# The store of the relative-bias rows is issued one weight piece later in the SyncE order

## The chip, the cores and the metric

The program runs on one core of one Trainium2 chip. The metric is device time in microseconds (us). Engines are TensorE (PE for its matmuls, PEld for its weight loads), VectorE (DVE), ScalarE (ACT), GpSimd (POOL) and SyncE (SP), which here only issues DMAs.

## What is computed

One layer of a hybrid decoder trunk on x of 512 tokens by 1024 channels, float32. The normalised input is multiplied by one wide projection `w_in`, whose columns feed three token mixers (A: sparse attention with a low-rank K/V and an indexer, B: gated DeltaNet, C: compressed, selected and window attention) and three merge gates. Their outputs go through `w_branch`, the gates and `w_out`, and are added to x. All softmax attention shares one relative-bias table:

```python
h = rms_norm(x, norm_g[l])
proj = h @ w_in[l]
a_part, b_part, c_part, gate_part = split_cols(proj, (...))
...
bias = jnp.transpose(bias_tab[t5_bucket(dist)], (0, 3, 1, 2))     # 32 buckets x 8 heads
logits = jnp.einsum('bqhd,bqkhd->bhqk', qb, kg) * scale + bias
...
x = x + (merged @ w_out[l])
```

## The kernel before

**Weights.** The projection is cut into chunks of up to 512 columns, and each chunk into four pieces (0 to 3), each with 2 of the 8 blocks of 128 rows (an exception are the two `phi` chunks, not touched here). The chunks at the start are C0 (448 columns), C1 (460), A0 (384), QI (512) and A2 (328), in that order, so the running piece number n is 0 to 3 for C0, 4 to 7 for C1, 8 to 11 for A0 and 12 to 15 for QI.

**The way of a piece.** SyncE loads piece n into one of three `stage` buffers (`load`, L449); from n = 3 on it first waits until the low split of piece n - 3 has been made (`lo_ready`), which is when that buffer comes free. ScalarE scales the piece in place (two ACTIVATEs, L738) and writes its float16 high part to `w_hi` (L746, which also waits for one of six `w_hi`/`w_lo` pairs to come free). GpSimd then writes the low part, `stage - w_hi`, to `w_lo` (L520). TensorE multiplies: a chunk is four tiles (t = 0 to 3), each tile eight k-steps of three matmuls (L1626, L1627, L1628: high by high, high by low, low by high), and k-steps 2j and 2j + 1 use piece j. So a tile has 24 matmuls and a chunk 96, and the first tile of a chunk waits for the low part of each of its pieces (`ready_pair`).

**Order on ScalarE.** Everything is in program order. `drain_chunk` copies a tile's bank out (L729) and then prepares pieces of the next chunk: after tile 0 its piece 0, after tile 1 its piece 1, after tile 2 its pieces 2 and 3, after tile 3 nothing (`FOLLOW`). The banks of the tiles alternate between two. GpSimd follows the same table; after the low splits of C1 it squares the C0 results (L537, L539).

**The relative-bias rows.** In the third gap of chunk C0 TensorE multiplies the table by a one-hot matrix (L1688, two products), VectorE scales the result into `rel_row` (8 partitions by 640 floats, L1086) and increments `rows_ready` (L1089). SyncE waits for this, stores the rows 16 times over to the DRAM tensor `rel_rows` (L480, 320 KB) and later, from piece QI,0 on, after the wait for `row_stored`, reads them back shifted into `strips` (L486, eight loads, one ahead of each of eight weight pieces). The other waits for `row_stored` and `strips_loaded` stand on VectorE ahead of the `ukv` copies in chunk A2 (L1177), on GpSimd (L615) and on VectorE (L1429), all later.

SyncE's queue is written out by hand: a wait in it holds back every load that stands behind it.

Of the kernel before, what the change touches and what calls it, by code (L numbers as in the profile page):

```python
# [127 lines left out]
def trunk(nc, x, norm_g, w_in, a_kv_norm, a_w_ukv, a_q_norm, a_k_norm, b_conv, b_a_log, b_dt_bias, b_out_norm,  # L128
# [9 lines left out]
    with ctx:  # L138
# [237 lines left out]
        for c, j in order:  # L376
            phi_piece = CHUNKS[c][0] == "phi"
            pieces.append((c, j, n_phi if phi_piece else n_pairs))
            n_phi, n_pairs = n_phi + phi_piece, n_pairs + (not phi_piece)
        piece_at = {(c, j): n for n, (c, j, _) in enumerate(pieces)}  # L380
        pair_at = {(c, j): k for c, j, k in pieces if CHUNKS[c][0] != "phi"}
        split_chunks = [c for c in range(len(CHUNKS)) if CHUNKS[c][0] != "phi"]
# [35 lines left out]
        def piece_view(t, c, n_rows=2):  # L418
            n = CHUNKS[c][2]
            return t[:, 0:n_rows * n].rearrange("p (k n) -> p k n", k=n_rows)  # L420
# [4 lines left out]
        @block.sync  # L425
        def _(sp):
            def load_x(t):
                sp.dma_start(x_in[t], x[0, t * P:(t + 1) * P, :]).then_inc(x_loaded[t], 16)

            def twice(row):  # L430
                return row.unsqueeze(1).to_broadcast([row.shape[0], 2, 64])

            def halves(row, n):
                return par_rows[row:row + n, :].rearrange("r (a d) -> r a d", a=2)

            def load(n):
                c, j, k = pieces[n]
                src, c0, width = CHUNKS[c]
                if n >= STAGES:
                    pc, _, pk = pieces[n - STAGES]  # L440
                    sp.wait_ge(phi_used if CHUNKS[pc][0] == "phi" else lo_ready, pk + 1)
                if src == "phi":
                    dst = piece_view(stage[:, n % STAGES, :], c, 4)
                    ap = c_phi_w1[0, c0].rearrange("(k p) n -> p k n", p=P)[:, 4 * j:4 * j + 4, :]
                else:
                    dst = piece_view(stage[:, n % STAGES, :], c)
                    ap = {"w_in": w_in, "w_branch": w_branch, "w_out": w_out}[src][0].rearrange(
                        "(k p) n -> p k n", p=P)[:, 2 * j:2 * j + 2, c0:c0 + width]
                sp.dma_start(dst, ap).then_inc(w_loaded[n % STAGES], 16)  # L449

            load_x(0)
            load_x(1)
            load(0)
            load(1)
            load_x(2)
            load_x(3)
            load(2)
            for src, dst in (
                (b_conv[0].rearrange("w (m p) -> (w m) p", p=P), par_rows[R_CONV:R_CONV + 48, :]),
                (a_kv_norm, par_rows[R_CKV:R_CKV + 1, :]),  # L460
                (twice(a_q_norm), halves(R_AQ, 1)), (twice(a_k_norm), halves(R_AK, 1)), (twice(c_q_norm), halves(R_CQ, 1)),
                (twice(c_k_norm[0]), halves(R_CK, 3)),
                (b_out_norm, par_rows[R_BOUT:R_BOUT + 1, :]),
                (c_cmp_pos[0].rearrange("v (c a) d -> (v c) (a d)", a=2), par_rows[R_POS:R_POS + 32, :]),
            ):
                sp.dma_start(dst, src).then_inc(in_loaded, 16)
            for src, dst in (
                (floats[:, F_HOT:F_HOT + S_REL], hot),
                (rel_bias, rel33[0:N_BUCKETS, :]),
                (b_dt_bias.to_broadcast([P, 4]), dt_b), (b_a_log.to_broadcast([P, 4]), neg_exp_a),  # L470
                (c_phi_w2[0].rearrange("v (k p) n -> p (v k) n", p=P), phi2),
            ):
                sp.dma_start(dst, src).then_inc(const_loaded, 16)
            sp.dma_start(ukv, a_w_ukv[0]).then_inc(ukv_loaded, 16)

            for n in range(STAGES, piece_at[CH_WO0, 0]):
                if n == piece_at[CH_C1, 3]:

                    sp.wait_ge(rows_ready, 1)
                    sp.dma_start(rel_rows, rel_row.unsqueeze(1).to_broadcast([N_HEADS, ROW_COPIES, S_REL])).then_inc(row_stored, 16)  # L480
                h = n - piece_at[CH_QI, 0]
                if 0 <= h < P // ROW_COPIES:

                    if h == 0:
                        sp.wait_ge(row_stored, 16)
                    sp.dma_start(strips[ROW_COPIES * h:ROW_COPIES * (h + 1), :, :],  # L486
                                 bass.AP(rel_rows.tensor, P - 1 - ROW_COPIES * h,
                                         [[S_REL - 1, ROW_COPIES], [ROW_COPIES * S_REL, N_HEADS], [1, T]])).then_inc(strips_loaded, 16)
                if n == piece_at[CH_A0, 2]:
                    sp.dma_start(mask_halves, masks).then_inc(masks_loaded, 16)  # L490
                load(n)

            sp.wait_ge(y_ready, NT * 2)
            sp.dma_start(x_again, x[0].rearrange("(t p) d -> p t d", p=P)).then_inc(x_reloaded, 16)
            for n in range(piece_at[CH_WO0, 0], len(pieces)):
                load(n)
            for n in range(2):
                for t in range(NT):
                    sp.wait_ge(out_ready, NT * n + t + 1)
                    sp.dma_start(out[0, t * P:(t + 1) * P, 512 * n:512 * n + 512],  # L500
                                 x_again[:, t, 512 * n:512 * n + 512]).then_inc(out_stored, 16)
            sp.wait_ge(out_stored, 16 * 2 * NT)
# [1585 lines left out]
```

## Time and profile before

| | us |
|---|---|
| median of 3 runs | 647.11 |
| the three runs | 2108.56, 643.32, 647.11 |
| profiled execution, its own time | 644.06 |
| span of its trace | 641.9 |
| mean granted TensorE clock, share of full speed | 0.981 |

The span is what the instructions cover; 2.2 us of the profiled execution's own time lie around it. Times in the rows below count from the start of the span.

### The profile page before, as it was taken

The page shows a single profiled execution, that of the slowest core. Times are in us where ns is not written, and L with a number is a line of the kernel's source. Part 1 is how long each engine was busy: PE and PEld are TensorE (multiplying, and loading weights), DVE is VectorE, ACT ScalarE, POOL GpSimd, SP SyncE. Part 2 cuts the span into 40 slices and gives each one's busy share as a digit, 9 for nine tenths or more (in the row PEclk, how much of TensorE's full clock was granted, in tenths as well). Part 3 has the DMA queues.
Part 4 walks back from the last instruction along what each step waited for, and adds up shares of the span by engine and source line. Part 5 has one row for each costly group of instructions (what it writes and reads, how often), then busy time and mean ns, then how long its engine had stood idle before and what let it go on. Part 6 is the DMA issues. An engine that isn't in the chain of part 4 may idle for free.

```text
span 641.9 us, 10022 instructions
## 1 busy us (share of the span) xinstructions
PE 585.5 (91%) x3763; PEld 365.5 (57%) x3763; DVE 395.0 (62%) x894; ACT 324.8 (51%) x578; POOL 222.7 (35%) x161
## 2 busy tenths in 40 slices
PE   3969997999999988799999999999999898799997
PEld 2424555756547754577777777765555555333443
DVE  6401477461577985886886556628799786477311
ACT  4634654434688868450712413257676767244510
POOL 0133452352225384142433430233313473132520
PEclk9998998999999899799999999999999999999999
DMA  8254783554213331220211020121111221072411
GB/s 321 70 127 110 152 135 99 149 148 130 67 26 83 124 100 34 66 66 2 62 37 34 13 88 1 34 67 51 54 63 34 67 66 46 21 242 83 135 50 49
DMA packets 31168, 53.04 MB, mean 83 GB/s; under 512 B 2743, under 2 KB 13201, under 8 KB 31121
## 3 DMA queue, kind: packets, MB, share of 16 engines
q1 hardware_dynamic: 30961, 52.27, 28.4%
q8 instruction: 30, 0.49, 0.3%
q14 instruction: 17, 0.14, 0.1%
q10 hardware_dynamic: 160, 0.14, 0.1%
HBM read 49.98 MB, written 2.42 MB: 82 GB/s over the span
## 4 chain that ended last, share of the span: by engine, by line
PE 68%; DVE 13%; ACT 8%; issue 5%; DMA 2%; POOL 2%; SPq 2%; DVEq 0%; ACTq 0%; POOLq 0%
PE bank L1813 13%; PE bank L1626 11%; PE bank L1628 10%; PE bank L1627 10%; PE bank L1885 5%; PE bank L1881 5%; PE bank L1883 5%; ACT stage L738 3%; DMA stage<-in_w_in 2%; PE bank L1662 2%; POOL w_lo L520 2%; PE bank L1705 2%; PE bank L2011 1%; ACT w_hi L746 1%; PE bank L1784 1%
## 5 line engine op out<-in xcount | busy, mean ns | idle before, releaser
L520 POOL TENSOR_TENSOR w_lo<-stage,w_hi 128x1024 f16<-128x1024 f32 (+4 forms) x76 | 149.1, 1963 | 242.4 <-ACT w_hi L746 242.4
L1813 PE MATMUL bank<-work 128*128 128x128 f32 x616 | 79.6, 279 | 8.1 <-DVEq L1319 7.9
L1813 PEld LDWEIGHTS bank<-work 128*128 128x128 f32 x616 | 76.8, 193 | 16.7 <-DVEq L1319 9.9
L746 ACT ACTIVATE w_hi<-stage 128x1024 f16<-128x1024 f32 (+4 forms) x76 | 74.5, 981 | 21.1 <-issue 17.2
L738 ACT ACTIVATE stage<-stage,small 128x512 f32<-128x512 f32 (+4 forms) x120 | 73.6, 662 | 7.8 <-DMA stage<-in_w_in 7.7
L1881 PE MATMUL bank<-hT_hi,w_hi 128*128 128x512 f16 x192 | 73.3, 382 | 1.7 <-PE bank L1885 0.9
L1883 PE MATMUL bank<-hT_lo,w_hi 128*128 128x512 f16 x192 | 73.3, 382 | 0.5 <-PE bank L1628 0.5
L1885 PE MATMUL bank<-hT_hi,w_lo 128*128 128x512 f16 x192 | 73.1, 381 | 0.3 <-PE bank L1628 0.2
L1626 PE MATMUL bank<-w_hi,hT_hi 128*128 128x260 f16 (+4 forms) x192 | 62.8, 327 | 9.4 <-POOL w_lo L520 6.4
L1627 PE MATMUL bank<-w_lo,hT_hi 128*128 128x260 f16 (+4 forms) x192 | 62.6, 326 | 0.0
L1628 PE MATMUL bank<-w_hi,hT_lo 128*128 128x260 f16 (+4 forms) x192 | 62.4, 325 | 0.0
L1626 PE MATMUL bank<-hT_hi,w_hi 128*128 128x512 f16 (+1 forms) x128 | 47.4, 371 | 6.2 <-DVE work L1140 3.8
L1344 DVE COPY_PREDICATED work<-level_masks,bank 128x512 f32<-128x512 uint8 x48 | 35.2, 734 | 23.6 <-PE bank L1813 17.4
L1628 PE MATMUL bank<-hT_hi,w_lo 128*128 128x512 f16 (+1 forms) x128 | 47.4, 370 | 0.0
L1627 PE MATMUL bank<-hT_lo,w_hi 128*128 128x512 f16 (+1 forms) x128 | 47.2, 369 | 0.0
L913 ACT ACTIVATE late<-late,small 128x128 f32<-128x128 f32 (+3 forms) x48 | 26.8, 557 | 30.7 <-DVE small L1427 30.7
L763 ACT ACTIVATE early<-bank 128x512 f32<-128x512 f32 x12 | 7.1, 591 | 61.8 <-PE bank L1885 61.8
L1626 PEld LDWEIGHTS bank<-w_hi,hT_hi 128*128 128x128 f16 x192 | 19.6, 102 | 24.4 <-POOL w_lo L520 7.3
L1227 DVE SCALAR_TENSOR_TENSOR bank<-qkvT,par,bank 128x512 f32<-128x512 f32 x36 | 27.0, 755 | 7.6 <-ACT bank L828 6.1
L1626 PE MATMUL bank<-strips,w_hi 128*128 128x512 f16 x64 | 25.1, 392 | 4.3 <-DVE strips L1533 1.5
L1881 PEld LDWEIGHTS bank<-hT_hi,w_hi 128*128 128x128 f16 x192 | 19.0, 99 | 15.7 <-issue 4.2
L1885 PEld LDWEIGHTS bank<-hT_hi,w_lo 128*128 128x128 f16 x192 | 18.9, 98 | 14.5 <-issue 2.0
(322 smaller groups left out, 1173.5 us busy)
## 6 DMA issues: line engine op xcount, KB each, us to landing
stage<-in_w_in SPq DMA_DIRECT2D x40, 512.0 KB, 3.5
stage<-in_c_phi_w SPq DMA_DIRECT2D x8, 512.0 KB, 3.9
stage<-in_w_branch SPq DMA_DIRECT2D x8, 512.0 KB, 3.7
stage<-in_w_out SPq DMA_DIRECT2D x8, 512.0 KB, 3.8
stage<-in_w_in SPq DMA_DIRECT2D x8, 260.0 KB, 2.8
strips<-rel_rows SPq DMA_DIRECT2D x8, 256.0 KB, 6.7
late<-in_x SPq DMA_DIRECT2D x1, 2048.0 KB, 10.3
out_x<-late SPq DMA_DIRECT2D x8, 256.0 KB, 2.0
```

Of the source, the lines that this page charges most:

```text
L520: gp.tensor_tensor(piece_view(w_lo[:, k % PAIRS, :], c), piece_view(stage[:, piece_at[c, j] % STAGES, :], c), piece_view(w_hi[:, k % PAIRS ...
L738: ins = nc.scalar.activation(full[:, r, :], full[:, r, :], ACT.Copy, scale=g_w[:, 2 * j + r:2 * j + r + 1])
L746: nc.scalar.activation(piece_view(w_hi[:, k % PAIRS, :], c), full, ACT.Copy).then_inc(hi_ready, 1)
L1227: ins = ve.scalar_tensor_tensor(acc, qkvT[:, m, w:w + T], tap[w], acc, ALU.mult, ALU.add)
L1344: return ve.copy_predicated(dst, level_masks[:, n, :].unsqueeze(1).to_broadcast([P, 4, P]), src)
L1626: mm(ps, lhs[0], rhs[0], start=start, stop=False)
L1627: mm(ps, lhs[0], rhs[1], start=False, stop=False)
L1628: return mm(ps, lhs[1], rhs[0], start=False, stop=stop)
L1813: ins = mm(ps[:, h * P:(h + 1) * P], lhs(h), rhs(h), start=True, stop=True)
L1881: mm(G.bank(g)[:, :], w[0], h[0], start=k == 0, stop=False)
L1883: mm(G.bank(g)[:, :], w[0], h[1], start=False, stop=False)
L1885: ins = mm(G.bank(g)[:, :], w[1], h[0], start=False, stop=k == KC - 1)
```

## The change

The wait for `rows_ready` and the store stood ahead of the load of piece 7, which is (C1, 3). They now stand ahead of the load of piece 8, which is (A0, 0). Nothing else differs, and no instruction is added or removed.

```diff
             for n in range(STAGES, piece_at[CH_WO0, 0]):
-                if n == piece_at[CH_C1, 3]:
+                if n == piece_at[CH_A0, 0]:
 
                     sp.wait_ge(rows_ready, 1)
                     sp.dma_start(rel_rows, rel_row.unsqueeze(1).to_broadcast([N_HEADS, ROW_COPIES, S_REL])).then_inc(row_stored, 16)
```

SyncE's order from piece 6 on was: load 6, wait and store, load 7, load 8, load 9, masks, load 10, load 11, first strip load, load 12. It is now: load 6, load 7, wait and store, load 8, and so on.

## Rows read from the trace of the kernel before

**Rows 1.** The page: TensorE's busy share, and the chain's shares.

```profile
PE 585.5 (91%) x3763; PEld 365.5 (57%) x3763; DVE 395.0 (62%) x894; ACT 324.8 (51%) x578; POOL 222.7 (35%) x161
...
PE 68%; DVE 13%; ACT 8%; issue 5%; DMA 2%; POOL 2%; SPq 2%; DVEq 0%; ACTq 0%; POOLq 0%
```

**Rows 2.** TensorE's waits from 30 to 130 us: total, times, longest.

```profile
PE bank L1626 <- POOL w_lo L520: 5.7, 1, 5.7
PE bank L1626 <- DVE work L1140: 3.8, 1, 3.8
```

**Rows 3.** Timeline of TensorE, 38 to 67 us: start, duration, instruction.

```profile
38.49 0.35 PE L1626 MATMUL bank<-w_hi,hT_hi 128*128 128x460 f16 x1 [0.30 <-PE bank L1628]
...
41.80 0.36 PE L1628 MATMUL bank<-w_hi,hT_lo 128*128 128x460 f16 x1
47.89 0.57 PE L1626 MATMUL bank<-w_hi,hT_hi 128*128 128x460 f16 x1 [5.73 <-POOL w_lo L520]
...
65.45 0.36 PE L1628 MATMUL bank<-w_hi,hT_lo 128*128 128x460 f16 x1
66.11 0.32 PE L1626 MATMUL bank<-w_hi,hT_hi 128*128 128x384 f16 x1 [0.30 <-PE bank L1628]
```

**Rows 4.** Timeline of GpSimd: low splits of pieces 4, 6, 7 and 8.

```profile
26.40 1.93 POOL L520 TENSOR_TENSOR w_lo<-stage,w_hi 128x920 f16<-128x920 f32 x1 [7.48 <-ACT w_hi L746]
...
35.92 1.93 POOL L520 TENSOR_TENSOR w_lo<-stage,w_hi 128x920 f16<-128x920 f32 x1 [2.13 <-ACT w_hi L746]
45.91 1.92 POOL L520 TENSOR_TENSOR w_lo<-stage,w_hi 128x920 f16<-128x920 f32 x1 [8.06 <-ACT w_hi L746]
...
52.92 1.64 POOL L520 TENSOR_TENSOR w_lo<-stage,w_hi 128x768 f16<-128x768 f32 x1 [2.67 <-ACT w_hi L746]
```

**Rows 5.** Timeline of ScalarE: pieces 6 and 7, a drain, piece 8.

```profile
34.87 0.97 ACT L746 ACTIVATE w_hi<-stage 128x920 f16<-128x920 f32 x1 [0.79 <-ACT stage L738]
43.58 1.25 ACT L738 ACTIVATE stage<-stage,small 128x460 f32<-128x460 f32 x2 [7.74 <-DMA stage<-in_w_in]
44.86 0.97 ACT L746 ACTIVATE w_hi<-stage 128x920 f16<-128x920 f32 x1
...
50.41 0.55 ACT L729 ACTIVATE raw_c<-bank 128x460 f32<-128x460 f32 x1 [4.14 <-PE bank L1628]
50.86 1.11 ACT L738 ACTIVATE stage<-stage,small 128x384 f32<-128x384 f32 x2
52.00 0.84 ACT L746 ACTIVATE w_hi<-stage 128x768 f16<-128x768 f32 x1
```

**Rows 6.** SyncE's own waits, 0 to 110 us.

```profile
SPq L480 <- DVEq L1089: 15.0, 1, 15.0
```

**Rows 7.** Timeline of SyncE: the store and loads 7 to 9.

```profile
34.15 0.75 SPq L480 DMA_DIRECT2D rel_rows<-work  x1
34.94 6.27 SPq L449 DMA_DIRECT2D stage<-in_w_in  x3
```

**Rows 8.** L449 from 34 to 50 us (four loads): issue durations, landing times.

```profile
L449 SPq DMA_DIRECT2D stage<-in_w_in x4: 368/1660/2864, 34.9 to 47.9; - x4
...
DMA to landing us min/median/max: 3.2/7.9/9.2
```

**Rows 9.** The DMA view, by line and size.

```profile
stage<-in_w_in SPq DMA_DIRECT2D x4, 460.0 KB, 4.2
```

**Rows 10.** Windows: length, busy us (count) by engine, PEclk, DMA share, GB/s.

```profile
30.00:32.00 2.00, 2.00 (x12) 1.02 (x11) 0.49 (x1) 1.75 (x3) 0.14 (x1) 1.00 0.00 0
...
42.20:47.90 5.70, 0.01 (x1) 0.01 (x1) 0.00 (x0) 2.65 (x4) 1.99 (x2) 0.86 0.57 211
47.90:53.20 5.30, 5.30 (x14) 2.09 (x15) 1.66 (x2) 2.40 (x4) 2.63 (x3) 0.50 0.26 74
...
101.00:104.40 3.40, 3.40 (x14) 2.07 (x13) 1.37 (x4) 2.26 (x4) 2.46 (x2) 0.51 0.23 61
...
258.00:264.80 6.80, 4.17 (x14) 2.72 (x15) 6.34 (x11) 2.96 (x5) 1.50 (x2) 0.50 0.44 146
```

## The prediction, made before the result was known

> **What bounds the kernel now.** I read the page first: TensorE is busy 91% of the span and holds 68% of the chain that ended last [rows 1]. A change to a DMA order can therefore pay only where TensorE stands still and waits, directly or through other engines, for what that order delays. TensorE's waits in the stretch around the store show one such place: a single wait of 5.7 us for a low split by GpSimd, the longer of the two of note there [rows 2]. The timeline places it between 41.80, the start of the 18th matmul of chunk C1, and 47.89 [rows 3]: tile 0 has used pieces 4, 5 and 6 (18 matmuls) and lacks piece 7.
>
> Then I followed piece 7 backwards. Its low split runs from 45.91, with GpSimd idle for 8.06 us before it [rows 4]; ScalarE idles 7.74 us before scaling it at 43.58 and names the DMA into `stage` [rows 5]; the load that brings it is the first of three issued from 34.94, right behind the store at 34.15 [rows 7]; and SyncE had waited 15.0 us, from 19.15 on, for VectorE's `rows_ready` [rows 6]. So SyncE was idle when piece 7 could first have been fetched. Its buffer is the one of piece 4, whose low split ended at 26.40 + 1.93 = 28.33 [rows 4], and the DMA engines moved nothing at all at that time: 0 GB/s from 30 to 32 us [rows 10].
>
> The pause costs twice. The granted clock after it is 0.50 from 47.9 to 53.2, 1.2 GHz in place of 2.4, with 14 matmuls in 5.30 us [rows 10].
>
> **The change, step by step.** *Load 7.* It is issued at about 28.4 instead of 34.94, 6.5 us sooner, and has an idle queue ahead of it instead of the store. It took 43.58 - 34.94 = 8.6 us to land [rows 5, 7]; the median of the four loads of its size is 4.2 us [rows 9]. I take 4.2, since no other transfer is under way, hence 32.6; with 8.6 it would be 37.0.
>
> *ScalarE and GpSimd.* ScalarE is done with piece 6 at 34.87 + 0.97 = 35.84 [rows 5], so for a landing at 32.6 the DMA is no longer what comes last; ScalarE's order is. Piece 7: scale 1.25, high part 0.97, together 2.25 with the gap between them [rows 5], to about 38.1; low split 1.92 [rows 4], to about 40.1. TensorE needs it after 18 matmuls of C1. These start at 38.49 and 41.80 for the first and 18th, a pitch of 3.31 / 17 = 0.195 us, so the need is at 38.49 + 18 x 0.195 = 42.0 [rows 3]. That leaves 1.9 us of cover. With the late landing of 37.0 the low split would end at 41.2, still in time; the cover is gone for a landing after about 37.8, and from there each us costs one.
>
> *TensorE.* The 96 matmuls of C1 then run in one go: 38.49 + 95 x 0.195 = 57.0 for the start of the last one, against 65.45 [rows 3]. The difference is 8.5 us. By parts: the pause removed, 5.7 [rows 2]; the half clock removed: 14 matmuls in 5.30 us instead of 14 x 0.195 = 2.73, which is 2.6 [rows 3, 10]; 8.3 together, the rest is the ends of the two pieces. I take 8.5.
>
> *The wait and the store.* `rows_ready` comes at the same time, since TensorE and VectorE do the same until then, so the store stays at 34.15: SyncE's order, wait for VectorE included, now holds back load 8 instead of load 7. Load 8 could have gone from 34.94 on at best before; it was issued right after load 7, so at 34.94 it is 0.5 us sooner than before. It now lands behind the store: with the largest landing of the four loads there, 9.2 us, at 44.1 [rows 7, 8]. Who waits for it: ScalarE, after the drain of tile 0 of C1. That tile ends with its 24th matmul, at about 38.49 + 24 x 0.195 = 43.2, plus the drain of 0.55 [rows 3, 5], so 43.8. In the worst of these cases ScalarE waits 0.3 us, and its order then holds back the drain of tile 1 by no more. What is needed on TensorE is piece 8 at 57, and the bank of tile 1 at 38.49 + 72 x 0.195 = 52.5. So it costs nothing.
>
> *Behind load 8 on SyncE.* Load 9, the masks, load 10. The three loads took 6.27 us to issue, where the shortest issue takes 0.37 [rows 7, 8]: while the store drains, the queue pushes back. One load fewer is issued in that time, so I expect this to be no worse. Load 9 is wanted at about 48.4 (tile 1's end) and load 10 at 53, while all three loads had been issued by 34.94 + 6.27 = 41.2 [rows 7]. The strip loads follow load 11, which waits for the low split of piece 8, and that moves with TensorE: it began at 52.92 [rows 4], and should begin near 43.8 + 1.95 = 45.8, by scale and high part of piece 8 [rows 5]. The store has had from 34.15 on to land, over 12 us. The value for all of them is zero; the bound from above is 0.3 us for load 8.
>
> *A rule beside this.* Load 7 took 8.6 us behind the store, twice the 4.2 of its size [rows 5, 7, 9]. The Trainium skill, "DMA: Bandwidth & Descriptors", section "Why a DMA increments its semaphore by 16 and not by 1", says that the slowest dimension of an access pattern sets over how many DMA engines a transfer is spread, which would be 8 of 16 for this store. It speaks against the change: the store taxes whatever stands behind it, now load 8. By that rule the tax stays in full and the gain could be 0.3 us smaller, 8.2; without a tax load 8 would land at 34.94 + 4.2 = 39.1 and the gain be 8.5.
>
> *What is late next.* Nothing in sight up to A0: the pieces of A0 hang on the drains of C1, and these move with TensorE by the same 8.5 us. In the 100 us after it I find no wait for a DMA on TensorE (its other wait there is 3.8 us for VectorE [rows 2], whose work hangs on TensorE's transposes), so the gain should be handed through.
>
> **Sum.** The profiled execution took 644.06 us; less 8.5 it is 635.6. The median of the three runs, 647.11, stands 3.1 above it, and the lowest, 643.32, stands 0.7 below; as one of the three is far out, I place the kernel before at 644 to 645 and the changed one at 636. The change is 1.3%, inside the 2% that is about what a measurement of this kernel tells from none.
>
> **Rivals.** *The clock takes a part back, or adds to it.* After other pauses the granted clock also stands at 0.50 to 0.51, for 3.4 us at 101.0 and for 6.8 at 258.0 [rows 10]. In a kernel that runs 8.5 us sooner these may appear, vanish or double. A stretch of 3.4 us filled with matmuls does 1.7 us of work, so it costs 1.7; one of 6.8 with 4.17 busy costs about 2.1. One more of them gives 637 to 638, two more 640; one fewer 634. For it: TensorE pauses in the stretches ahead of these, as the 3.8 us wait [rows 2] ahead of 101.0. Against: the pauses keep their lengths, so there is no reason for more of them in sum. The Trainium skill, "TensorE: Matmul & The Clock Gate", section "Part 1: The HAM clock gate (the "warmup" mystery)", says that the change of clock is not tied to the kernel's start and that its place varies from run to run; the trace can't show this in one execution. By that rule the size of the second term, 2.6, is a draw of each execution, and the first term stands alone in the worst case, which gives 644.1 - 5.7 = 638.4. Chance that the net is worse than 638.5: 13%.
>
> *Nothing is gained.* Piece 7 would be waited for by another cause as well, such as its `w_hi` pair or GpSimd. Against it: the 7.74 us are put down to the DMA, piece 6's high part at 34.87 shows the pair wait ending then, and GpSimd idles 8.06 us. Also the edit might not do what it says, if load 7 were not issued before 34. Its only wait is for the low split at 28.33. 643 to 646, chance 4%.
>
> *Slower: load 8 blocks ScalarE.* ScalarE takes its instructions in order, so a load 8 that lands late behind the store holds back the drains of C1 and with them the banks. It decides from a landing after about 50.0 (52.5 less drain 0.55, less scale and high part 1.95 [rows 5]), that is 15 us after the issue, against 9.2 for the longest here [rows 8]. To eat the whole gain it must land at 58.5, and 6.5 us later still would be a loss of 1%: 650. Chance 2%.
>
> *More than forecast.* The 3.4 us stretch at 101.0 goes too, and another: 631 to 633, chance 8%.
>
> **How the numbers follow.** The forecast, 633 to 638.5, has 73%. The range reaches to the edge of the clock's rival, two stretches more, and takes in the spread of the medians (643.32 to 647.11 for the same kernel, 3.8 us): 631 to 642. It leaves out the no-gain case, the slower one and a few per cent on either side. Faster by over 2% needs 13 us or a low draw of the noise: 5%. Slower by over 2%: 2%. Within 2%: 93%.
>
> **What would show it.** SyncE: a load of `stage` at about 28.4, and the wait for L1089 shortened from 15.0 to some 5.4 us. ScalarE: no wait of note for the DMA before piece 7. TensorE: the 5.7 us wait of L1626 for L520 absent, clock 1.00 through 38 to 57, the first A0 matmul at 57.5 instead of 66.11. Later landmarks all 8.5 earlier. It is wrong if a wait for L520 stays between 38 and 58, if a wait of ScalarE for the DMA of more than a few us stands before piece 8, or if the landmarks' lead shrinks behind 100 us.

## The result, and the profile after

The changed kernel took 637.04 us, median of four runs (635.15 to 639.34). Its ratio to the kernel before is 0.9883 with a 95% interval of 0.9851 to 0.9914, so it is 1.2% faster, clear of noise and inside 2%. That ratio is the one of the means, 637.14 and 644.66, so the gain is 7.5 us, with 5.5 to 9.6 by the interval. The medians give less: a fourth run of the kernel before took 643.54, and 643.54 less 637.04 is 6.5. The profiled execution took 635.15 us, with a span of 633.1 against 641.9 and a mean granted clock of 0.987 against 0.981. The run of the kernel before of 2108.56 us is left out of all of these. Beside the experiments the kernel before ran 32 times more, with medians of 644.46 (e1 to e4) and 644.08 (e5 to e8).

The instruction order of the two kernels is the same on TensorE, VectorE, ScalarE and GpSimd. Only SyncE's differs.

SyncE, its waits from 0 to 110 us, against [rows 6]. The wait for VectorE is 5.4 us instead of 15.0:

```profile
SPq L480 <- DVEq L1089: 5.4, 1, 5.4
```

SyncE, timeline (start, duration, instruction), against [rows 7]:

```profile
28.13 0.37 SPq L449 DMA_DIRECT2D stage<-in_w_in  x1
33.91 0.75 SPq L480 DMA_DIRECT2D rel_rows<-work  x1
34.71 3.36 SPq L449 DMA_DIRECT2D stage<-in_w_in  x2
38.11 2.86 SPq L490 DMA_DIRECT2D late<-in_masks  x1
41.02 6.65 SPq L449 DMA_DIRECT2D stage<-in_w_in  x2
```

Load 7 is the row at 28.13, alone; the store follows at 33.91. The store stood at 34.15 before: this whole execution is 0.24 us ahead of that one before the change can act (the low split of piece 4 starts at 26.17 instead of 26.40). Executions of the other kernels below differ by as much and more, so this offset is taken off below.

The landing of load 7 (L449, 28 to 29 us) and of load 8 behind the store (34 to 35.2 us), against [rows 8]:

```profile
DMA to landing us min/median/max: 3.2/3.2/3.2
...
DMA to landing us min/median/max: 8.4/8.4/8.4
```

So piece 7 was there at 31.3, and the late landing has passed to piece 8, which came at 43.1.

ScalarE, timeline: pieces 6 and 7, the last drain of C0, the first drain of C1, piece 8, against [rows 5]:

```profile
34.64 0.97 ACT L746 ACTIVATE w_hi<-stage 128x920 f16<-128x920 f32 x1 [0.79 <-ACT stage L738]
35.52 1.23 ACT L738 ACTIVATE stage<-stage,small 128x460 f32<-128x460 f32 x2
36.78 0.97 ACT L746 ACTIVATE w_hi<-stage 128x920 f16<-128x920 f32 x1
38.00 0.54 ACT L729 ACTIVATE early<-bank 128x448 f32<-128x448 f32 x1 [0.25 <-PE bank L1628]
43.13 0.56 ACT L729 ACTIVATE raw_c<-bank 128x460 f32<-128x460 f32 x1 [4.59 <-PE bank L1628]
43.58 1.11 ACT L738 ACTIVATE stage<-stage,small 128x384 f32<-128x384 f32 x2
```

The bracket names the wait. Piece 7 is scaled right behind piece 6, with no wait for a DMA; the 7.74 us of before are gone. Piece 8 landed at 43.1, as ScalarE was beginning the drain ahead of it, and was scaled right behind that drain: the landing was just in time for ScalarE.

GpSimd, the low split of piece 7, against [rows 4]; it ends at 39.76:

```profile
37.83 1.93 POOL L520 TENSOR_TENSOR w_lo<-stage,w_hi 128x920 f16<-128x920 f32 x1 [0.20 <-ACT w_hi L746]
```

TensorE, timeline, against [rows 3]; then its longest wait from 30 to 130 us, against [rows 2]:

```profile
38.27 0.35 PE L1626 MATMUL bank<-w_hi,hT_hi 128*128 128x460 f16 x1 [0.30 <-PE bank L1628]
...
41.57 0.36 PE L1628 MATMUL bank<-w_hi,hT_lo 128*128 128x460 f16 x1
41.76 0.36 PE L1626 MATMUL bank<-w_hi,hT_hi 128*128 128x460 f16 x1
...
57.40 0.32 PE L1626 MATMUL bank<-w_hi,hT_hi 128*128 128x384 f16 x1 [0.30 <-PE bank L1628]
```

```profile
PE bank L1626 <- DVE work L1140: 3.8, 1, 3.8
```

Between the 18th matmul (41.57) and the 19th (41.76) there is no gap, and no wait of L1626 for L520 is listed. A0 starts at 57.40 instead of 66.11: 8.71 us, or 8.47 without the offset.

The windows view (length; busy us and count of PE, PEld, DVE, ACT, POOL; PEclk; DMA share; GB/s), against [rows 10]:

```profile
42.20:47.90 5.70, 5.70 (x31) 2.87 (x30) 1.66 (x2) 2.51 (x5) 1.64 (x1) 1.00 0.51 191
47.90:53.20 5.30, 5.30 (x29) 2.63 (x27) 0.00 (x0) 3.03 (x6) 1.64 (x1) 1.00 0.67 131
91.80:95.20 3.40, 3.40 (x14) 1.87 (x13) 1.66 (x4) 2.42 (x4) 1.79 (x2) 0.52 0.29 101
```

In the first window TensorE was idle before and now runs without a gap (5.70 us busy, 31 matmuls in it or reaching into it). In the second it ran 14 at 1.2 GHz and runs 29 at 2.4. The stretch at half clock that stood at 101.0 is still there, at 91.8.

The lead is handed through. The products of `phi` (L1705) begin at 101.6 instead of 110.3, those of L1813 on `work` at 252.0 instead of 260.6, the transposes of the probabilities (L2011) at 415.8 instead of 424.6: 8.7, 8.6 and 8.8 us. These two executions have their later stretches at half clock in the same places of the program; where they lie elsewhere (e3, e8), single landmarks don't keep a lead so evenly.

### The profile page after: what moved, and what is told of

It is laid out like the page before. It is cut to its first block, busy times and chain, and to the rows that moved or that the text cites. A ratio compares the mean times of both kernels' runs of the same rounds, so it can differ in the third digit from the quotient of the medians.

```text
span 633.1 us, 10022 instructions
## 1 busy us (share of the span) xinstructions
PE 582.9 (92%) x3763; PEld 365.2 (58%) x3763; DVE 394.9 (62%) x894; ACT 324.9 (51%) x578; POOL 222.7 (35%) x161
## 4 chain that ended last, share of the span: by engine, by line
PE 70%; DVE 13%; ACT 8%; issue 4%; POOL 2%; SPq 1%; DMA 1%; DVEq 0%; ACTq 0%; POOLq 0%
PE bank L1813 13%; PE bank L1626 11%; PE bank L1628 10%; PE bank L1627 10%; PE bank L1885 5%; PE bank L1881 5%; PE bank L1883 5%; ACT stage L738 3%; PE bank L1662 2%; PE bank L1705 2%; POOL w_lo L520 2%; PE bank L2011 1%; PE bank L1784 1%; DVE work L1344 1%; PE bank L1844 1%
## 5 line engine op out<-in xcount | busy, mean ns | idle before, releaser
L520 POOL TENSOR_TENSOR w_lo<-stage,w_hi 128x1024 f16<-128x1024 f32 (+4 forms) x76 | 149.1, 1964 | 234.1 <-ACT w_hi L746 234.1
L1813 PE MATMUL bank<-work 128*128 128x128 f32 x616 | 79.6, 279 | 8.1 <-DVEq L1319 7.8
L1813 PEld LDWEIGHTS bank<-work 128*128 128x128 f32 x616 | 76.8, 193 | 16.7 <-DVEq L1319 9.9
L1626 PE MATMUL bank<-w_hi,hT_hi 128*128 128x260 f16 (+4 forms) x192 | 61.8, 322 | 3.3 <-DVE hT_lo L1051 1.4
L1626 PE MATMUL bank<-hT_hi,w_hi 128*128 128x512 f16 (+1 forms) x128 | 47.4, 370 | 6.4 <-DVE work L1140 3.8
L1344 DVE COPY_PREDICATED work<-level_masks,bank 128x512 f32<-128x512 uint8 x48 | 35.2, 734 | 23.5 <-PE bank L1813 17.4
L1626 PEld LDWEIGHTS bank<-w_hi,hT_hi 128*128 128x128 f16 x192 | 19.4, 101 | 16.9 <-issue 4.6
L1626 PE MATMUL bank<-strips,w_hi 128*128 128x512 f16 x64 | 25.0, 390 | 4.4 <-DVE strips L1533 1.5
L1881 PEld LDWEIGHTS bank<-hT_hi,w_hi 128*128 128x128 f16 x192 | 18.9, 98 | 15.6 <-issue 3.9
```

Of the source, the lines that this page charges most:

```text
L520: gp.tensor_tensor(piece_view(w_lo[:, k % PAIRS, :], c), piece_view(stage[:, piece_at[c, j] % STAGES, :], c), piece_view(w_hi[:, k % PAIRS ...
L1344: return ve.copy_predicated(dst, level_masks[:, n, :].unsqueeze(1).to_broadcast([P, 4, P]), src)
L1626: mm(ps, lhs[0], rhs[0], start=start, stop=False)
L1813: ins = mm(ps[:, h * P:(h + 1) * P], lhs(h), rhs(h), start=True, stop=True)
L1881: mm(G.bank(g)[:, :], w[0], h[0], start=k == 0, stop=False)
```

## The experiments

The experiments are called e1 to e8. The theory under test: piece 7 was late because its load stood behind a wait and a slow store; TensorE's pause cost its own length and, behind it, a stretch at half clock; and what TensorE gains at A0 arrives at the end. The main rivals are written in the expectations. Ratios are to the kernel before, timed beside it on the same chip.

**Only the store moves (e1).** The wait stays ahead of load 7.

```diff
                 if n == piece_at[CH_C1, 3]:
                     sp.wait_ge(rows_ready, 1)
+                if n == piece_at[CH_A0, 0]:
                     sp.dma_start(rel_rows, ...).then_inc(row_stored, 16)
```

> The wait for rows_ready stays ahead of load 7, the store alone moves behind it. It asks which of the two delayed piece 7: the store's traffic or SyncE's wait. Theory (both, and mostly the traffic): load 7 is issued at about 33.9 and lands after 3.2 to 4.2 us with no transfer ahead of it, at 37.1 to 38.1; scale and high part 2.25, low split 1.93, so piece 7 is ready at 41.3 to 42.3, against a need of TensorE at 41.8. Pause 0 to 0.6 us, clock at full speed, first A0 matmul at 57.4 to 58.0, time 0.987 to 0.989 of before, like the change. Rival (the wait alone did it, the traffic is harmless): load 7 is issued only 0.8 us sooner than before, so the first A0 matmul stays at 65 or later and the time within 0.3% of before.

Measured: 636.40 us, ratio 0.9869 (0.9842 to 0.9895). ScalarE, timeline, piece 7; GpSimd, its low split; TensorE, start of A0:

```profile
37.47 1.25 ACT L738 ACTIVATE stage<-stage,small 128x460 f32<-128x460 f32 x2 [1.71 <-DMA stage<-in_w_in]
```

```profile
39.79 1.93 POOL L520 TENSOR_TENSOR w_lo<-stage,w_hi 128x920 f16<-128x920 f32 x1 [2.03 <-ACT w_hi L746]
```

```profile
57.54 0.32 PE L1626 MATMUL bank<-w_hi,hT_hi 128*128 128x384 f16 x1 [0.30 <-PE bank L1628]
```

Load 7 was issued at 34.06, only 0.9 us sooner than before, landed 3.4 us later, and the low split ended at 41.72, just ahead of the 19th matmul at 41.91, with no pause listed on TensorE. So the wait in SyncE's queue alone costs nothing here: it uses up the slack. With the store ahead as well the piece comes 6.1 us later (43.58 against 37.47 on ScalarE): 5.2 of it are the landing, 8.6 against 3.4, and 0.9 the issue. The opposite case, an early issue with a store ahead of it, was not run.

**Load 7 late, no store ahead (e2).** The changed kernel, plus a hold on load 7.

```diff
+                if n == piece_at[CH_C1, 3]:
+                    sp.wait_ge(lo_ready, pair_at[CH_C1, 2] + 1)
                 if n == piece_at[CH_A0, 0]:
```

> The changed order, but load 7 is also held until the low split of piece 6 has ended (37.6), with no store ahead of it. It asks whether TensorE's pause follows the landing of piece 7 one for one. Theory: issue 37.7, landing 40.9 with 3.2 us, low split done at 45.1, pause of L1626 behind L520 of 3.3 us (3.2 to 4.3 by the landing); first A0 matmul at 60.7 with the clock kept, up to 63.3 if the half clock comes as well; time 0.991 to 0.997 of before. Rival (only the store's traffic matters, the issue has slack): no pause, first A0 matmul at 57.4, time 0.987.

Measured: 644.32 us, ratio 0.9966 (0.9942 to 0.999). TensorE, timeline around the pause and at the start of A0 (the lines of TensorE are two further down in this kernel):

```profile
41.53 0.36 PE L1630 MATMUL bank<-w_hi,hT_lo 128*128 128x460 f16 x1
45.57 0.49 PE L1628 MATMUL bank<-w_hi,hT_hi 128*128 128x460 f16 x1 [3.68 <-POOL w_lo L522]
```

```profile
62.90 0.32 PE L1628 MATMUL bank<-w_hi,hT_hi 128*128 128x384 f16 x1 [0.30 <-PE bank L1630]
```

Load 7 went at 37.61 and ScalarE took the piece at 41.27, 3.7 us later instead of 3.2, hence a pause of 3.68 instead of 3.3. A0 starts 5.5 us after the changed kernel's. The gap in TensorE's pitch gives 45.57 - 41.53 - 0.195 = 3.85 of it; behind the pause the granted clock was 0.53 for 3.5 us with 10 matmuls, which take 1.95 us at full speed, so 1.55 more. A late issue without the store did as much harm as its lateness past the cover, one for one, plus the clock: a landing 3.5 us after the 37.8 of the prediction, a pause of 3.7. This execution took 645.07 us, one of the slower of two groups of runs, which the last section shows; the rest of its loss lies in later stretches at half clock.

**The pause filled with matmuls (e3).** The kernel before, with TensorE kept busy.

```diff
+            def within_c1(t, k):
+                if (t, k) == (0, 5):
+                    for _ in range(29):
+                        mm(banks[7][:, 0:460], hT_hi[:, 0, 0:P], part(CH_C1, 0, 0, 460)[0], start=True, stop=True)
-            project(CH_C1, "C1", True)
+            project(CH_C1, "C1", True, within=within_c1)
```

> The order of before, with 29 matmuls of 460 columns into an unused bank put between the 18th and 19th matmul of C1, where TensorE paused; they add work of 29 x 0.195 = 5.66 us, whose result is not read. It prices the clock's part. Theory: piece 7 comes as before (low split done at 47.8), the clock stays at full speed behind it, and the first A0 matmul comes at 47.9 + 78 x 0.195 + 0.5 = 63.5 instead of 66.1: 2.6 us faster than before, 0.996. Rival (the half clock was not due to the pause, or is not on the path): granted clock 0.50 behind 47.9 again, A0 at 66.1, time 1.000.

Measured: 642.11 us, ratio 0.9963 (0.9941 to 0.9985). The windows of the filled pause and of the stretch behind it, then the start of A0:

```profile
42.50:48.40 5.90, 5.81 (x30) 2.74 (x28) 0.00 (x0) 2.65 (x4) 1.95 (x2) 1.00 0.58 213
48.40:53.80 5.40, 5.37 (x28) 2.74 (x29) 2.93 (x2) 2.40 (x4) 3.88 (x3) 1.00 0.27 76
```

```profile
64.08 0.32 PE L1626 MATMUL bank<-w_hi,hT_hi 128*128 128x384 f16 x1 [0.30 <-PE bank L1628]
```

The clock stayed at 1.00 where it had been 0.50. The store of this execution is at 34.67, 0.52 us after the 34.15 of before, so A0 starts at 63.56 by that clock against 66.11: 2.55 us, where 2.6 was predicted. The half clock is due to the pause, and is its own term of the sum. More work on TensorE made the kernel faster: 2.4 us by the ratio. Further on the lead of this one execution isn't steady. It is 3.6 us at the products of `phi` (106.7 against 110.3), 0.2 at those of L1813 (260.4 against 260.6) and 2.4 at the end of the span (639.5 against 641.9), as later stretches at half clock lie elsewhere; that the gain arrives rests on the ten runs.

**Two stores ahead of load 8 (e4).**

```diff
                     sp.dma_start(rel_rows, ...).then_inc(row_stored, 16)
+                    sp.dma_start(rel_rows2, ...).then_inc(row_stored, 16)
...
-                        sp.wait_ge(row_stored, 16)
+                        sp.wait_ge(row_stored, 32)
```

> The changed kernel with a second store of the same rows to another DRAM tensor right behind the first, so twice the slow traffic ahead of load 8; the waits ask for both. It measures the cover of load 8. Theory (covered): load 8 lands at about 34.7 + 0.8 + 8.4 + 6 = 49 to 50 instead of 43.1; ScalarE waits some 5 to 6 us for it, the masks and loads 9 and 10 come later as well, TensorE doesn't wait for L520 more than 1 us, and the time is that of the changed kernel, 0.987 to 0.991 of before. Rival (no cover, each us counts): first A0 matmul 5 to 6 us later than 57.4, time 0.996 or more.

Measured: 636.66 us, ratio 0.987 (0.9836 to 0.9903). ScalarE, timeline, piece 8 and the drain of tile 1 behind it (its lines are one further down here); then the start of A0 on TensorE:

```profile
49.81 1.12 ACT L739 ACTIVATE stage<-stage,small 128x384 f32<-128x384 f32 x2 [5.84 <-DMA stage<-in_w_in]
50.96 0.84 ACT L747 ACTIVATE w_hi<-stage 128x768 f16<-128x768 f32 x1
51.71 0.54 ACT L730 ACTIVATE raw_c<-bank 128x460 f32<-128x460 f32 x1
```

```profile
57.67 0.32 PE L1627 MATMUL bank<-w_hi,hT_hi 128*128 128x384 f16 x1 [0.30 <-PE bank L1629]
```

Load 8 landed 14.1 us after its issue, at 49.8, ScalarE lost 5.84 us to it, and A0 starts where it did, at 57.67 (the store is at 34.16 here, so 57.42 by the changed kernel's clock). The drain of tile 1 ends at 51.71 + 0.54 = 52.25, just ahead of the 52.5 at which tile 3 begins (38.27 + 72 x 0.195, and 0.25 for the later start). From A0 on later pieces came late, with waits for L521 of 2.1 us in all, the longest 1.5. The time doesn't show them: the wait for VectorE behind them (L1141 here) is 2.2 us instead of 3.8, and the products of `phi` begin at 101.0, no later than the 101.6 of the changed kernel.

**Three stores ahead of load 8 (e7).** As e4, with a third `sp.dma_start(rel_rows3, ...)` and waits for 48.

> The changed kernel with three stores instead of one ahead of load 8, to three DRAM tensors. It carries load 8 past the end of its cover, which I put at a landing of 50. Theory (cover, then one for one, through ScalarE's order and the banks): load 8 lands at 55.3 to 56, ScalarE drains tile 1 of C1 at about 58, TensorE pauses 5 to 6 us ahead of tile 3 (from 52.3), the half clock adds up to 2.6, and pieces 9 to 11 come late as well; first A0 matmul at 63 to 68, time 0.997 to 1.005 of before. Rival (the cover is larger, as with the doubled store): time within 0.3% of the changed kernel.

Measured: 645.85 us, ratio 1.0018 (1.0002 to 1.0033). ScalarE's wait, and TensorE's timeline at tile 3 of C1 and at A0:

```profile
55.94 1.12 ACT L740 ACTIVATE stage<-stage,small 128x384 f32<-128x384 f32 x2 [12.31 <-DMA stage<-in_w_in]
```

```profile
58.43 0.56 PE L1628 MATMUL bank<-w_hi,hT_hi 128*128 128x460 f16 x1 [6.07 <-ACT raw_c L731]
65.50 0.32 PE L1628 MATMUL bank<-w_hi,hT_hi 128*128 128x384 f16 x1 [0.30 <-PE bank L1630]
```

Here the slower rival of the prediction shows. TensorE waits 6.07 us for a drain (L731) that stood in ScalarE's order behind a piece that TensorE needed only 7 us later. With the half clock that followed, another 1.9 us (11 matmuls from 58.43 to 62.51, where 2.15 would do), A0 starts 8.1 us late and the whole gain is gone. The end of the cover lies between landings of 49.8 and 55.9; the pause of 6.07 behind the landing at 55.9 puts it at 49.9, where the prediction had 50.0.

**The store one piece further on again (e5).**

```diff
-                if n == piece_at[CH_A0, 0]:
+                if n == piece_at[CH_A0, 1]:
```

> Wait and store one piece further on again, ahead of load 9, (A0, 1). It asks whether anything is left to gain by the place in SyncE's queue. Theory (the changed kernel has no wait for these loads left on TensorE): load 8 is issued when the low split of piece 5 ends, at about 33.6, and lands at about 37 instead of 43; ScalarE wants it at 43.6 only, so the first A0 matmul stays at 57.4 and the time at that of the changed kernel, 0.987 to 0.990 of before. Rival (load 8 behind the slow store still costs): up to 1 us faster than the changed kernel.

Measured: 636.59 us, ratio 0.9875 (0.9855 to 0.9894), A0 at 57.30. Load 8 was issued at 33.5 and landed in 3.2 us, at 36.7, 6.4 us sooner than in the changed kernel, and that bought nothing.

**The store issued by GpSimd (e6).** Out of SyncE's queue altogether.

```diff
+                if t == 2:
+                    lo_split(CH_C1, 2)
+                    gp.wait_ge(rows_ready, 1)
+                    gp.dma_start(rel_rows, ...).then_inc(row_stored, 16)
+                    lo_split(CH_C1, 3)
+                    continue
                 follow(CH_C0, t)
```

> Wait and store are taken out of SyncE's queue and issued by GpSimd, behind the low split of piece 6 (36 to 38 us). It asks whether it is the wait and store in the loads' queue that matters. Theory: SyncE has no wait for VectorE; load 7 is issued at about 28.1, the store at about 37.7 beside the loads; GpSimd's issue takes up to 1 us, so piece 7's low split ends at 39.8 to 41, in time for 41.6; no pause, first A0 matmul at 57.4, time 0.987 to 0.991 of before. Rival (the store slows the loads from any queue, or its issue on GpSimd costs over 2 us): a pause of L1626 behind L520 of over 0.5 us comes back.

Measured: 636.43 us, ratio 0.9889 (0.9854 to 0.9924). GpSimd, timeline (the low split is line 516 here), and SyncE, the masks:

```profile
37.50 0.77 POOL L532 DMA_DIRECT2D rel_rows<-work  x1
38.30 1.94 POOL L516 TENSOR_TENSOR w_lo<-stage,w_hi 128x920 f16<-128x920 f32 x1
```

```profile
37.99 0.47 SPq L486 DMA_DIRECT2D late<-in_masks  x1
```

The issue cost GpSimd 0.77 us, piece 7 was ready at 40.24, and A0 starts at 57.36. Once the store isn't ahead of piece 7, none of the three places tried for it is better than another. The masks took 0.47 us to issue here, and 3.56 in e5, where SyncE issued them at the same time (37.97) with the store ahead in its own queue: the slow issue came with the store in that queue.

**2.9 us more work on TensorE (e8).** The changed kernel with e3's filler, 15 instead of 29.

> The changed kernel with 15 matmuls of 460 columns into an unused bank behind the 18th matmul of C1, whose result is not read: 15 x 0.195 = 2.9 us more work for TensorE, no pause, no change of clock there. It asks whether a us on TensorE in this stretch is a us at the end. Theory (handed through): first A0 matmul at 60.3, and the time 2.9 us above the changed kernel, within the 2 us by which the later stretches at half clock differ from run to run: 0.989 to 0.995 of before. Rival (absorbed later, by the waits for VectorE that are there anyway): the lead is back by the token-major products of A2, and the time is that of the changed kernel, 0.987.

Measured: 639.52 us, ratio 0.9918 (0.9892 to 0.9944). TensorE at the start of A0:

```profile
60.42 0.32 PE L1626 MATMUL bank<-w_hi,hT_hi 128*128 128x384 f16 x1 [0.30 <-PE bank L1628]
```

A0 is 3.0 us later than in the changed kernel, and the time is 3.0 us above the 636.5 of e5 and e6, which ran beside it. Within the 2 us or so by which runs differ, a us in this stretch is a us at the end. (The profiled executions alone show it less cleanly: 6.4 us later than the changed kernel's at L1813, 4.2 at the end of the span.) The waits for VectorE behind it took up little: the one of 3.8 us at L1140 is 3.3 here.

## Why the prediction was right

*The bound.* One pause of TensorE, followed back to one load: right. Of the other places tried for the store none mattered (e5, e6).

*Load 7.* Issue 28.4 predicted, 28.13 measured (28.37 with the offset). The landing took 3.2 us, not 4.2: the median of [rows 9] has load 7 itself in it, at 8.6 behind the store. The cover was large enough for either.

*ScalarE and GpSimd.* The prediction took the 0.79 us ahead of the high part of piece 6 for the wait for its `w_hi` pair; the bracket there names only ScalarE's own scaling, so this is a reading of the program, not of the row. The high part of piece 7 follows at 36.78 with no wait in front of it, so the pair did not hold it. Low split of piece 7 done at 40.1 predicted, 39.76 measured, for a need at 41.76. Cover of 1.9 us predicted, 2.0 measured. That the cover ends at a landing of about 37.8 is borne out by e1 (landing at 37.5, no pause) and e2 (41.3, a pause of 3.7).

*TensorE.* 8.5 us predicted at A0, 8.47 measured. The parts: pause 5.7, and half clock 2.6 against the 2.55 of e3. The second is no constant: behind the pauses of e2 and e7 (3.7 and 6.1 us) it was 1.55 and 1.9.

*Load 8.* Landing no later than 44.1 predicted, 43.1 measured, at no cost. The tax of the store stayed in full, 8.4 us to land against 3.2 with nothing ahead (e5), but it fell where there was cover. I expected the issues behind the store to be no worse, and they were a little better: before, loads 8 and 9 took 2.86 us each to issue; now they took 0.46 and 0.42, and the masks 2.86 instead of 0.47. Load 10 went at 41.02, 1.3 us after its buffer came free. The slower rival was rightly built and its cover rightly measured: one store more is free (e4). Its price was too low. It put the loss of the whole gain at a landing of 58.5, one for one from 50.0, and left out the half clock; in e7 a landing at 55.9 was enough.

*Handed through.* 8.7, 8.6 and 8.8 us at three later landmarks, and e8 at the end.

*The sum.* 8.5 forecast; 7.5 measured between the means (5.5 to 9.6), 6.5 between the medians, and 8.91 between the two profiled executions (644.06 and 635.15), of which 0.24 is the offset. 636 was forecast and 637.04 came. The profiled execution of the changed kernel is the fastest of its four, so of the two figures the 8.91 flatters the forecast. The base of 644 to 645, put below the 647.11 of the three runs, was right by the later medians of 644.46 and 644.08. The half clock rival was real as a spread, not as a loss: the changed kernel's four runs have a mean granted clock from 0.987 (635.15 us) to 0.978 (639.34 us).

*Imprecise.* The prediction names two things that bring piece 7 sooner, an issue 6.5 us earlier and no store ahead, and doesn't say which is needed. By e1 the second is enough, if only just: an issue 0.9 us earlier with the store behind it gives the same time. By the prediction's own sum the first would be enough too (37.0, with the landing of 8.6, against 37.8); no run shows that. The change has both, and so more than it needs.

## What to carry to other kernels

In a hand-written DMA queue, find for each transfer the engine whose order it stops, and put a slow one behind the last load whose cover is shorter than its drain; here 2 us of cover stood ahead of it and 7 us behind. Price a pause of TensorE with the half clock that followed it: 2.6 us on top of 5.7 here, 1.55 on 3.7 in e2, 1.9 on 6.1 in e7. A load can hurt through an in-order engine long before its own data are needed: piece 8 was wanted by TensorE at 57, but stopped a drain that was wanted at 52.

## What the runs showed that I had not expected

**The store is slow, and the queue behind it is slow to issue too.** From the first store's issue to the landing of load 8 it took 9.2 us with one store, 15.6 with two (34.16 to 49.8) and 22.1 with three (33.85 to 55.9): 6.4 to 6.5 us for each 320 KB, or some 50 GB/s, where a load of 460 KB landed 3.2 us after its issue. That it is slow because it reads only 8 partitions was not tried. Behind three stores, L449 from 37 to 47 us:

```profile
L449 SPq DMA_DIRECT2D stage<-in_w_in x2: 4552/4570/4589, 40.0 to 44.7; - x2
...
DMA to landing us min/median/max: 12.3/14.1/15.9
```

SyncE stands 4.6 us in the issue of one load (0.37 with an idle queue). So a slow transfer held back not only the data behind it but the engine that issues.

**Later stretches at half clock differ between executions of one kernel.** The ten runs of e2 fall into two groups, 640.5 to 641.8 and 643.9 to 645.1 us. Its profiled execution had lost 5.5 us against the changed kernel at the start of A0, and 8.8 by the products of L1813 (260.8 against 252.0), with a mean clock of 0.976 against 0.987. Why one execution gets more such stretches was not tried; it sets the 2 us or so on either side below which single runs of this kernel say nothing.
